# Feed-forward stages linked by semaphore waits in place of hand-overs, with the first weights of the next stage prepared early and a second raw buffer for the short block

## The reference, cut to what matters

```python
def swiglu(h, w_in, w_out):
    gate, up = jnp.split(h @ w_in, 2, axis=-1)
    return (jax.nn.silu(gate) * up) @ w_out
...
hl = modulate(rms_norm(xl, g[2]), mod_l[3], mod_l[4])
xl = xl + mod_l[5] * rms_norm(swiglu(hl, ffn_w_in[l], ffn_w_out[l]), g[3])
```

## Time and profile before

| what | value |
|---|---|
| median of 3 runs | 4217.67 us (4212.2 to 4218.17) |
| the profiled execution, its own time | 4221.19 us |
| its span, first to last instruction | 4219.4 us |
| TensorE busy with matmuls, share of the span | 3569.6 us, 85% |
| mean granted TensorE clock, share of 2.4 GHz | 0.92 |
| layer 0, first block: `hidden`, `project_back` | 254.60 us, 131.45 us |
| layer 0, second block: `hidden`, `project_back` | 251.79 us, 131.04 us |
| layer 0, short block: `hidden`, `project_back` | 161.94 us, 123.45 us |
| layer 1, first block: `hidden`, `project_back` | 252.13 us, 131.89 us |

### The profile page before, as it was taken

The page is one execution under the profiler, slowest core; times in us unless marked ns, Lnnn a source line. Parts: engine busy times, 40 slices in busy tenths (PEclk is TensorE's granted clock), DMA queues, the critical chain, the costliest instruction groups (busy, mean ns, idle before and its releaser), DMA issues. The chain is left out here.

```text
span 4219.4 us, 56278 instructions
## 1 busy us (share of the span) xinstructions
PE 3569.6 (85%) x20754; PEld 2940.9 (70%) x20754; DVE 1755.9 (42%) x2494; ACT 1594.7 (38%) x2693; POOL 541.4 (13%) x929
## 2 busy tenths in 40 slices
PE   4998786896769999999886899767986779999997
PEld 3997454774558877877786799544774658787876
DVE  3112655776334522532452211555776345323322
ACT  3011455775233422422442211445775234223222
POOL 0001363121001100100100000444221011000000
PEclk8999886998889999999998899978998889999999
DMA  4224411004214323323443123612003133233323
GB/s 172 90 69 146 161 57 44 8 7 164 95 61 139 104 84 110 114 80 101 152 137 107 65 90 107 221 53 61 8 5 132 40 109 115 81 97 130 95 82 107
DMA packets 145410, 401.03 MB, mean 95 GB/s; under 512 B 15696, under 2 KB 79888, under 8 KB 138384
## 3 DMA queue, kind: packets, MB, share of 16 engines
q1 hardware_dynamic: 112848, 328.45, 24.2%
q0 software_dynamic: 11712, 43.00, 2.8%
q10 hardware_dynamic: 20736, 28.18, 1.9%
HBM read 337.32 MB, written 57.02 MB: 93 GB/s over the span
## 5 line engine op out<-in xcount | busy, mean ns | idle before, releaser
L759 PE MATMUL psum<-part,part 128*128 128x512 f32 (+2 forms) x4240 | 1526.8, 360 | 225.0 <-DVE part L1690 218.5
L760 PE MATMUL psum<-part,part 128*128 128x512 f32 (+2 forms) x4240 | 1515.9, 358 | 0.0
L761 PE MATMUL psum<-part,part 128*128 128x512 f32 (+2 forms) x4240 | 1514.7, 357 | 0.0
L759 PEld LDWEIGHTS psum<-part,part 128*128 128x128 f32 x4240 | 815.2, 192 | 335.4 <-issue 223.1
L1690 DVE TENSOR_TENSOR part<-region,part 128x1024 fp32r<-128x1024 f32 (+5 forms) x446 | 562.7, 1263 | 1111.7 <-ACT part L1572 546.2
L760 PEld LDWEIGHTS psum<-part,part 128*128 128x128 f32 x4240 | 815.3, 192 | 94.7 <-issue 1.0
L761 PEld LDWEIGHTS psum<-part,part 128*128 128x128 f32 x4240 | 814.1, 192 | 94.7
L1572 ACT CAST part<-region 128x1024 fp32r<-128x1024 f32 x220 | 230.5, 1048 | 488.9 <-PE psum L761 434.3
L2023 DVE TENSOR_REDUCE region<-psum 128x1 f32<-128x1280 f32 (+1 forms) x216 | 295.1, 1369 | 168.0 <-PE psum L1012 168.0
L1545 ACT CAST part<-region 128x1408 fp32r<-128x1408 f32 (+1 forms) x96 | 126.7, 1319 | 464.2 <-DMA region<-in_ffn_out 360.7
L1455 ACT ACTIVATE region<-psum,region 128x1280 f32<-128x1280 f32 (+1 forms) x216 | 266.7, 1235 | 92.2 <-DVE region L2023 91.9
(11 more groups left out here) (221 smaller groups left out, 3257.0 us busy)
## 6 DMA issues: line engine op xcount, KB each, us to landing
region<-in_ffn_in SPq DMA_DIRECT2D x220, 512.0 KB, 3.6
region<-in_ffn_out SPq DMA_DIRECT2D x80, 704.0 KB, 4.0
region<-in_ada_w SPq DMA_DIRECT2D x14, 2048.0 KB, 9.7
proj<-region ACTq DMA_DIRECT2D x16, 1720.0 KB, 11.3
region<-proj SPq DMA_DIRECT2D x20, 1376.0 KB, 8.8
region<-in_w_in SPq DMA_DIRECT2D x16, 1376.0 KB, 7.2
region<-in_ada_w SPq DMA_DIRECT2D x20, 1024.0 KB, 6.3
region<-proj SPq DMA_DIRECT2D x116, 128.0 KB, 2.3
```

The source lines that it names most:

```text
L759: mm(out, a[0], b[0], start=start, stop=False)
L760: mm(out, a[0], b[1], start=False, stop=False)
L761: return mm(out, a[1], b[0], start=False, stop=stop)
```

## The change

1. The hand-over between `hidden` and `project_back` goes away in all five blocks, and so does the one between `project_back` and the next block's `hidden`, of which there are three (two in layer 0, one in layer 1). The hand-overs at both ends of a feed-forward sub-layer stay.
2. Into `project_back`: SP loads the first unit once the last gate half is done (`gate_made`), instead of behind the hand-over. ScalarE casts it (`unit_hi`) before the last product's cast, VectorE makes its rest (`unit_lo`) before the last product. TensorE waits on a new semaphore `act_ready`, which counts the hidden tiles whose hi and lo are both there: the first 11 for `j = 0`, all 22 for `j = 1`.
3. Into the next `hidden`: SP loads the gate weights of tile 0 once the last unit's weights have been split, and the up weights once the last unit but one is multiplied. ScalarE and VectorE split the gate half before they keep the last output tile (`half_hi`, `half_lo`), and the up half after it.
4. `sum_y` moves behind tile 0 on TensorE, with a wait for the last sum of squares.
5. `project_back` of a feed-forward block accumulates in PSUM banks 2 and 3 (before: 0 and 3), since bank 0 now belongs to the next stage.
6. The short block has a second raw buffer, in the half of `ACT_HI` that 256 tokens leave free. `single` is 0 there, so SP may load unit m when unit m-2 has been split. The activations are packed by `n` instead of 512. The buffers' places at `W_AT` change.
7. GpSimd's stages of a sub-layer follow one another without hand-overs.

```diff
+        def y_bank(block, s):
+            return psum[:, (3 * s if block is None else 2 + s) * BANK:]
         def unit_slots(w_at, block, size):
 
-            second = w_at + 5 * size if block is None else w_at
-            return [w_at, second], [w_at + (1 + i) * size for i in range(2)], [w_at + (3 + i) * size for i in range(2)]
+            second = w_at + 5 * size if block is None else w_at if block[2] == FFN_T else ACT_HI + KH * block[2]
+            at = (1, 2, 3, 4) if block is None else (1, 3, 2, 4)
+            return [w_at, second], [w_at + i * size for i in at[0:2]], [w_at + i * size for i in at[2:4]]
...
-        WF = [[W_AT + (3 * half + i) * KD * P for i in range(3)] for half in range(2)]
-        SILU_AT = W_AT + 6 * KD * P
+        WF = [[W_AT + i * KD * P for i in range(3)], [W_AT + 3 * KD * P, W_AT + 3 * UNIT, W_AT + 3 * UNIT + KD * P]]
+        SILU_AT = W_AT + 3 * UNIT + 2 * KD * P
...
+                if block is not None:
+                    sp.wait_ge(sem("gate_made"), (block[0] + 1) * KH + 1)
...
-                handover("sp", sp)
+                if block is None or not after(l, block):
+                    handover("sp", sp)
 
             def hidden(l, block):
-                with sp.Fori(0, KH) as u:
+                units = back(l, block)[5]
+                sp.wait_ge(sem("wb_ready"), units + 2)
+                for u in range(2):
                     for half in range(2):
+                        if u == 0 and half == 1:
+                            sp.wait_ge(sem("yb_made"), units + 1)
                         sp.wait_ge(sem(f"wf_ready{half}"), block[0] * KH + u + 1)
                         sp.dma_start(region(WF[half][0], KD * P), t["ffn_in"][l, u, half]
                                      ).then_inc(sem(f"wf_in{half}"), 16)
-                handover("sp", sp)
+                with sp.Fori(2, KH) as u:
+                    for half in range(2):
+                        sp.wait_ge(sem(f"wf_ready{half}"), block[0] * KH + u + 1)
+                        sp.dma_start(region(WF[half][0], KD * P), t["ffn_in"][l, u, half]
+                                     ).then_inc(sem(f"wf_in{half}"), 16)
 
...
                             pe.wait_ge(sem("wb_ready"), units + per * (2 * u + s) + j + 3)
+                            if block is not None:
+                                pe.wait_ge(sem("act_ready"), block[0] * KH + (j + 1) * kk)
                             if j == 0:
 
                                 pe.wait_ge(sem("yb_kept"), chunks + 2 * u + s + 1)
                             for a, m in pieces:
-                                out = psum[:, 3 * s * BANK + a - first:3 * s * BANK + a - first + m]
+                                out = y_bank(block, s)[:, a - first:a - first + m]
...
                     if r.is_ffn:
+                        units(done, w_.y_rooted)
+                        done = w_.y_rooted
+                        pe.wait_ge(sem("sq_added"), back(l, block)[6] + 1)
                         sum_y(r)
...
+            def unit_hi(l, block, c, j, slot):
+                per, kk, _, _, w_at, units, _, _, _ = back(l, block)
+                raw, hi, _ = unit_slots(w_at, block, kk * P)
+                m = units + per * c + j
+                act.wait_ge(sem(f"wb_in{slot}"), 8 * (m - slot) + 16)
+                act.wait_ge(sem("yb_made"), m + 1)
+                nc.scalar.copy(region_r(hi[slot], kk * P), region(raw[slot], kk * P)).then_inc(sem("wb_hi"), 1)
+            def half_hi(l, block, u, half):
+                index = block[0]
+                if u == FIRST:
+                    act.wait_ge(sem("yb_made"), back(l, block)[5] + 1 + half)
+                act.wait_ge(sem(f"wf_in{half}"), 16 * (index * KH + u + 1))
+                act.wait_ge(sem("up_made" if half else "gate_made"), index * KH + u + 1)
+                nc.scalar.copy(region_r(WF[half][1], KD * P), region(WF[half][0], KD * P)
+                               ).then_inc(sem(f"wf_hi{half}"), 1)
...
+                following = block and after(l, block)
+                if following:
+                    half_hi(l, following, FIRST, 0)
                 keep(KD - 1, 1)
-                handover("act", act)
+                if not following:
+                    handover("act", act)
 
...
                 gate(KH - 1)
+                unit_hi(l, block, 0, 0, 0)
                 product_part(KH - 1)
                 renew(KH - 1)
-                handover("act", act)
 
...
+                         ).then_inc(sem("act_ready"), 1)
...
+                unit_lo(l, block, 0, 0, 0)
                 product(KH - 1)
                 renew(KH - 1)
-                handover("dve", dve)
...
                 for block_ in blocks(l):
                     hidden(l, block_)
-                    idle()
+                idle()
```

More of the change, by code:

```diff
@@ L1100, in project_back @@
                 per, kk, src_at, _, w_at, units, chunks, t0, n = back(l, block)
-                src = [region_r(at, KD if per == 1 else KH, N if per == 1 else FFN_T) for at in src_at]
+                src = [region_r(at, KD if per == 1 else KH, N if per == 1 else n) for at in src_at]
                 pieces = spans(t0) if per == 1 else [(0, n)]
@@ L1119, in project_back @@
                             last.then_inc(sem("yb_made"), 1)
-                handover("pe", pe)
+                if block is None or not after(l, block):
+                    handover("pe", pe)
             def hidden(l, block):
@@ L1532, in finish @@
                 handover("act", act)
+            def unit_hi(l, block, c, j, slot):
[13 more added lines that the diff above has]
+                               ).then_inc(sem(f"wf_hi{half}"), 1)
             def project_back(l, block=None):
                 per, kk, _, dst_at, w_at, units, chunks, t0, n = back(l, block)
-                raw, hi, _ = unit_slots(w_at, block, kk * P)
                 def chunk(c, s, is_first):
                     for j in range(per):
[L1541 to L1546, removed]
+                        if block is None or j or not is_first:
+                            unit_hi(l, block, c, j, j if per == 2 else s)
                     if not is_first:
@@ L2121, in finish, with unit_lo, half_lo, chunk @@
                 handover("dve", dve)
+            def unit_lo(l, block, c, j, slot):
+                per, kk, _, _, w_at, units, _, _, _ = back(l, block)
+                raw, hi, lo = unit_slots(w_at, block, kk * P)
+                dve.wait_ge(sem("wb_hi"), units + per * c + j + 1)
+                rest(region_r(lo[slot], kk * P), region(raw[slot], kk * P), region_r(hi[slot], kk * P)
+                     ).then_inc(sem("wb_ready"), 1)
+            def half_lo(block, u, half):
+                dve.wait_ge(sem(f"wf_hi{half}"), block[0] * KH + u + 1)
+                raw, hi, lo = WF[half]
+                rest(region_r(lo, KD * P), region(raw, KD * P), region_r(hi, KD * P)
+                     ).then_inc(sem(f"wf_ready{half}"), 1)
             def project_back(l, block=None):
-                per, kk, _, _, w_at, units, chunks, t0, n = back(l, block)
-                raw, hi, lo = unit_slots(w_at, block, kk * P)
+                per, kk, _, _, _, _, chunks, t0, n = back(l, block)
                 total, new = (region(at, N)[:, t0:t0 + n] for at in squares_at(block))
-                def chunk(c, s):
+                def chunk(c, s, is_first=False):
                     for j in range(per):
-                        slot = j if per == 2 else s
-                        dve.wait_ge(sem("wb_hi"), units + per * c + j + 1)
-                        rest(region_r(lo[slot], kk * P), region(raw[slot], kk * P), region_r(hi[slot], kk * P)
-                             ).then_inc(sem("wb_ready"), 1)
+                        if block is None or j or not is_first:
+                            unit_lo(l, block, c, j, j if per == 2 else s)
                 def add(c):
@@ L2146, in project_back @@
                         add(2 * u + s - 1)
+                following = block and after(l, block)
+                if following:
+                    half_lo(following, FIRST, 0)
                 add(KD - 1)
-                handover("dve", dve)
+                if not following:
+                    handover("dve", dve)
             def hidden(l, block):
                 index, t0, n = block
-                def part(u, half):
-                    dve.wait_ge(sem(f"wf_hi{half}"), index * KH + u + 1)
-                    raw, hi, lo = WF[half]
-                    rest(region_r(lo, KD * P), region(raw, KD * P), region_r(hi, KD * P)
-                         ).then_inc(sem(f"wf_ready{half}"), 1)
                 def product(u):
```

43 lines of the change are left out of this document (21 added, 22 removed).

## The result

| | before | after |
|---|---|---|
| median of four runs, all on one chip | 4216.40 us | 4092.62 us |
| the profiled execution, span | 4219.4 us | 4091.1 us |
| TensorE busy, share of the span | 85% | 87% |
| mean granted clock | 0.920 | 0.928 |

The ratio is 0.9712, 95% interval 0.9693 to 0.9731: 124 us faster in the medians, 128.3 us in the two spans. The forecast was 4101 us, 116.5 us faster.

What follows compares the result with a forecast made beforehand. TensorE, 85% busy, loses time in border gaps, low-clock stretches and the short project_back's one raw buffer. 31.6 + 4.4 + 19.5 + 12.8 + 50.2 - 2 = 116.5 us off 4217.7 gives 4101 us, range 4088 to 4111 (chance 0.72).

Steps and rivals of the forecast that it cites:

- Hidden to back, full blocks: Four borders from hidden to project_back: TensorE idles 1.9 us in place of 9.7; 31.6 us won.
- Hidden to back, short block: Short block's border from hidden to project_back: idle 4.5 us in place of 8.89; 4.4 us won.
- Back to hidden: Three borders from project_back to the next hidden: 20.5 us of gaps vanish, 1.0 lost to late up weights; 19.5 us won.
- The clock: Half-clock stretches behind border gaps: six us won where gaps close, 6.8 where they shrink; together 12.8 us won.
- The short block's back: Short block's project_back: two raw buffers make TensorE the bound, 64.8 us in place of 115.0; 50.2 us won.
- The alternative, longer loads when two overlap: Short block's project_back: two loads in flight take 5.3 us each, making the stage some 6 us longer than the sum.
- Small losses: Later x loads cost 1 us in the short block's hidden, full blocks' raw chain 1 us; 2 us lost.
- the raw chain: Full blocks' project_back: a 7.3 us raw chain directly behind TensorE's 7.5 us per unit; 1 us lost, bounds 0 and 6.
- A: Short project_back stops at chain or clock: 4111 to 4124 us, chance 0.15; half clock throughout 4149, chance 0.04.
- B: Early preparation moves the wait: in-order ScalarE and VectorE queues keep some 5 us idle per border; 4125 us, chance 0.07.
- C: Slower: granted clock falls under unbroken load in feed-forward sub-layers; 124 us at half clock eats the 116.5 won; chance 0.02.

Runs made afterwards that it cites:

- the second comparison: The unaltered changed kernel run once more on the same chip as the kernel before: medians 4089.0 against 4212.8 us, ratio 0.97 to 0.9727.
- raw over raw: Against the changed kernel, project_back's first raw buffer laid only over hidden's two raw buffers, first unit loaded about 3 us earlier: 4077.6 us, ratio 0.967 to 0.9698.

## Why the prediction was right

The measured 4092.6 us lie within the range, 8 us below the forecast. In the second comparison the medians were 4212.8 and 4089.0 us, again 123.8 us apart. By the terms of the sum, from the two traces:

- **Hidden to back, full blocks.** Forecast 31.6 won. The starts on both sides were 10.09, 10.15, 10.45 and 10.05 us apart and are 2.40, 2.54, 2.49 and 2.38: 30.9 won. SP issued 0.30 us after Silu started, not 0.1. The prediction's proof that both engines are idle at 1510, the 5.09 us before the cast in the earlier trace rows, begins only at 1513.35. The reading itself was right: by the trace ScalarE is idle from 1507.16 to 1512.72 and VectorE from 1505.46 to 1512.00.
- **Hidden to back, short block.** Forecast 4.4; 9.17 us became 4.73: 4.4.
- **Back to hidden.** Forecast 19.5. The starts were 8.35, 8.25 and 8.45 us apart and are 0.23 three times, 24.4 won. The moved sum takes 0.87 us of TensorE's time in each (1641.25 to 1642.80 for three matmuls, less their 0.68), 2.6, and the late up half 0.7. That is 21.1 won. The two sum matmuls cost less inside a stream than the 1.12 us that they are shown with.
- **The clock.** Forecast 12.8, with two stretches of 1.6 us kept behind the four gaps. Two were kept, both of 8 matmuls:

```profile
1875.55:1878.91 3.36, 3.36 (x9) 2.59 (x8) 0.69 (x1) 0.50 (x2) 0.00 (x0) 0.51 0.62 208
...
3947.62:3950.98 3.36, 3.36 (x10) 2.65 (x9) 0.69 (x1) 0.49 (x1) 0.00 (x0) 0.51 0.70 216
```

  In 3.36 us of half clock 1.6 us are lost. With 10.0 us behind the four old gaps, 6.0 behind the other three and 3.1 kept, the term is 12.9 us. That two of four were kept is in part luck: the six profiles with such gaps had two, three or four.
- **The short block's back.** Forecast 64.8 us from 115.0, 50.2 won; it is 65.39, 49.6 won. TensorE is the bound, as worked out; the stretch at half clock lost 2.1 us in place of 1.4 (21 matmuls in 4.64 us). The 16 loads of the stage landed in 4.0 us in the median, 5.4 at most. The alternative, longer loads when two overlap, was not refuted: it hardly arose. TensorE's pace let the loads out mostly 3.96 us apart, one landing about as the next went out (overlaps under 1 us). Only the stage's first two went out 0.9 us apart, and these landed in 4.1 and 5.4 us. That is near the 5.3 us that the prediction worked out from the Trainium skill's page "DMA: Bandwidth & Descriptors" (Anatomy of one DMA), although that page's fit is for transfers issued by GpSimd and these are issued by SP. (By the prediction's own rows such loads would make the stage 5 us longer, not 6.)

```profile
DMA to landing us min/median/max: 3.9/4.0/5.4
...
DMA to landing us min/median/max: 4.1/4.7/5.4
```

  (all sixteen, and the first two alone)

- **Small losses.** Forecast 2 lost. Of these the raw chain was to lose 1 us over four blocks, and it did: in layer 1's first block two units were late, 0.70 and 0.42 us more than 0.23 from start to start. Its second and fifth loads took 5.2 and 5.1 us in place of 4.0, and the chain was then longer than TensorE's unit:

```profile
3590.71 0.39 PE L790 MATMUL psum<-part,part 128*128 128x512 f32 x1
3591.64 0.50 PE L788 MATMUL psum<-part,part 128*128 128x512 f32 x1 [0.55 <-DVE part L1736]
...
3614.64 0.49 PE L788 MATMUL psum<-part,part 128*128 128x512 f32 x1 [0.27 <-DVE part L1736]
```

  With raw over raw, three of the four full blocks' back stages take 119.45 us from first to last matmul, 527 x 0.2266 = 119.4, so nothing is lost there; the fourth, the same block, takes 120.18. The short block's `hidden` became 3.8 us shorter (153.87 to 150.06), not 1 us longer, although the moved sum and the late up half now stand in it; 1.7 us of that is half clock that no longer follows its start, and what made the rest is open. This part had the wrong sign.

The terms by gap and stage sum to 30.9 + 4.4 + 21.1 + 49.6 = 106.0. The other 14.6 of F's 120.6 us are clock and small parts, against 12.8 - 2 = 10.8 forecast: 12.9 of clock, and so 1.7 won where 2 lost were put. So inside the sub-layers the forecast was 4 us short, nearly all of it in the small parts; the misses of the other terms (0.7 and 0.6 too much, 1.6 too little) nearly cancel. The remaining miss of the profiled execution lies in O: over thirteen profiles it lies anywhere between 2400.6 and 2415.2 us, and the same kernel had 2407.4 and 2400.6, another 2415.2 and 2404.3. O's 7.7 us are within that. Whether the changed kernel is also a few us faster there on average, two profiles can't tell; that stays open.

**The rivals.** A (the short stage stops at its chain or the clock) fell: 65.4 us at clock 0.96. B (the preparation moves the wait) fell: the borders kept what was worked out, the last product's delay cost nothing. C (the clock falls under the unbroken load) fell: in the stage between the first two borders it is 1.00 throughout, and over the whole sub-layers, layer 0 and layer 1, it is 0.99 (before: 0.96 and 0.98).

```profile
1511.00:1630.00 119.00, 119.00 (x526) 98.54 (x526) 30.50 (x25) 29.05 (x31) 0.00 (x0) 1.00 0.33 104
...
1263.00:2216.15 953.15, 929.18 (x4764) 795.81 (x4764) 410.82 (x486) 354.21 (x462) 65.28 (x72) 0.99 0.38 123
3337.60:4068.70 731.10, 725.97 (x3172) 597.96 (x3172) 256.15 (x270) 219.44 (x266) 23.10 (x27) 0.99 0.32 104
```

That is also what the Trainium skill's page "TensorE: Matmul & The Clock Gate" (Part 1) has for one busy core, whose peak-current limiter one or two busy cores never trip; the runs, with one core at work, agree with it.

## What to carry to other kernels

A barrier between stages costs what it puts in order, far more than the meeting itself: here, replaced by waits with the same order, it gave 0.06 us at the first border and 0.15 on average over five, while the first load moved ahead gave 7.7. So ask of each stage border when the buffer under the next load comes free, and lay that buffer over whatever is done earliest. And compare a stage's load, cast and split chain with TensorE's time per unit for the shortest tile too: one buffer just covered the full blocks (7.3 us against 7.5, and no longer when a load took 5.2 us) and cost the half-size block 50 us.

## What the runs showed of the hardware

At the borders from `hidden` to `project_back` in the full blocks, where two starts of TensorE are 2.34 to 2.61 us apart between streams at full clock, half clock followed in 16 of 24 cases, in six profiles, and in 8 not; the same border of the same kernel had it in one profile and not in the other. Behind the thirteen starts 1.57 or 1.58 us apart inside `hidden` it never followed. A forecast can give such a stretch a chance and a price (about 8 matmuls, 1.6 us), but not a place.

The 704 KB loads of the short block's `project_back`, most of them issued 3.96 us apart, landed in 4.0 us in the median. Of two issued 0.9 us apart the second took 5.4 us in the changed kernel, and behind a load of `hidden` still under way the two took 6.5 and 7.3 us.
